# A two-block model on one NeuronCore: the order of high and low weight products in a unit

## What is computed

```python
u = hn @ e_w_in[j]                 # 2048 x 6144
mix = y @ e_w_out[j]               # 2048 x 2048
h = h + jax.nn.sigmoid(h @ ple_gate_w[i]) * pl
...
h = rms_norm(x, norm_g) @ w_in
return x + (y @ w_out).astype(x.dtype)
```

## Time and profile before

| | |
|---|---|
| median of 3 runs | 2110.85 us (2109.73 to 2111.03) |
| profiled execution | 2112.97 us |
| its span | 2111.2 us, 36924 instructions |
| TensorE busy, matmuls | 2087.3 us (99%), 11920 |
| weight loads | 1816.1 us (86%), 11920 |
| POOL busy | 1775.9 us (84%), 1393 |
| ACT busy | 1239.2 us (59%), 2221 |
| DVE busy | 1070.5 us (51%), 1848 |
| granted TensorE clock, mean | 0.997 |
| DMA | 377.72 MB, 179 GB/s in the mean |

### The profile page before, as it was taken

How to read it: one execution, slowest core, us unless ns; L and a number is a source line. 1 busy time by engine, 2 the same in 40 slices (tenths; PEclk the granted TensorE clock), 3 DMA queues, 4 the chain that set the end, 5 groups by cost and what they waited for, 6 DMA issues and landing times.

```text
span 2111.2 us, 36924 instructions
## 1 busy us (share of the span) xinstructions
PE 2087.3 (99%) x11920; PEld 1816.1 (86%) x11920; DVE 1070.5 (51%) x1848; ACT 1239.2 (59%) x2221; POOL 1775.9 (84%) x1393
## 2 busy tenths in 40 slices
PE   9999999999999999999999999999999999999997
PEld 8887888888888888888888988888888888878886
DVE  7567685345663256633466554405644651277612
ACT  6575457556555467765666465446655544476654
POOL 8799788999989987789898968897799889866786
PEclk9999999999999999999999999999999999999999
DMA  8555335555556554455566535564566656534464
GB/s 278 197 185 173 132 120 164 191 186 190 190 191 216 187 175 159 158 182 190 184 200 206 184 131 180 191 192 154 154 197 189 209 180 205 191 131 144 138 190 143
DMA packets 208226, 377.72 MB, mean 179 GB/s; under 512 B 23248, under 2 KB 29776, under 8 KB 207952
## 3 DMA queue, kind: packets, MB, share of 16 engines
q1 hardware_dynamic: 203904, 368.34, 54.3%
q10 hardware_dynamic: 4176, 7.53, 1.1%
HBM read 373.68 MB, written 2.10 MB: 178 GB/s over the span
## 4 chain that ended last, share of the span: by engine, by line
PE 82%; DVE 3%; POOL 1%; issue 0%; ACT 0%; ACTq 0%; DVEq 0%; POOLq 0%
PE ps L612 43%; PE ps L614 22%; PE ps L593 3%; PE ps L595 3%; PE ps L594 3%; PE ps L852 2%; PE ps L879 1%; POOL w_lo L516 1%; PE ps L864 1%; PE ps L602 1%; PE ps L604 1%; PE ps L603 1%; PE ps L811 0%; PE ps L584 0%; PE ps L801 0%
## 5 line engine op out<-in xcount | busy, mean ns | idle before, releaser
L516 POOL TENSOR_TENSOR w_lo<-raw,w_hi 128x512 fp32r<-128x512 f32 (+2 forms) x1370 | 1755.1, 1299 | 315.8 <-ACT w_hi L964 269.0
L964 ACT ACTIVATE w_hi<-raw 128x512 fp32r<-128x512 f32 (+1 forms) x1388 | 860.0, 627 | 737.7 <-PE ps L614 586.6
L612 PE MATMUL ps<-xa,w_hi 128*128 128x512 f32 x2576 | 882.1, 397 | 5.0 <-POOL w_lo L516 4.9
L612 PE MATMUL ps<-xb,w_hi 128*128 128x512 f32 x2016 | 704.2, 396 | 0.1
L614 PE MATMUL ps<-xa,w_lo 128*128 128x256 f32 x2576 | 661.9, 278 | 0.0
L614 PE MATMUL ps<-xb,w_lo 128*128 128x256 f32 x2016 | 553.6, 278 | 0.0
L612 PEld LDWEIGHTS ps<-xa,w_hi 128*128 128x128 f32 x2576 | 461.6, 188 | 91.2 <-issue 3.7
L614 PEld LDWEIGHTS ps<-xa,w_lo 128*128 128x128 f32 x2576 | 484.7, 188 | 29.9
L612 PEld LDWEIGHTS ps<-xb,w_hi 128*128 128x128 f32 x2016 | 377.4, 188 | 85.6 <-issue 0.6
L614 PEld LDWEIGHTS ps<-xb,w_lo 128*128 128x128 f32 x2016 | 379.0, 188 | 3.8
L1624 DVE TENSOR_SCALAR tb<-ps 128x512 f32<-128x512 f32 (+1 forms) x92 | 63.2, 687 | 253.0 <-PE ps L614 252.6
(11 more groups left out here) (372 smaller groups left out, 2124.7 us busy)
## 6 DMA issues: line engine op xcount, KB each, us to landing
raw<-w_gate_dram SPq DMA_DIRECT2D x128, 256.0 KB, 3.0
raw<-w_ogz_dram SPq DMA_DIRECT2D x128, 256.0 KB, 2.9
raw<-w_ein_dram SPq DMA_DIRECT2D x96, 256.0 KB, 3.1
raw<-w_evout_dram SPq DMA_DIRECT2D x80, 256.0 KB, 2.8
raw<-w_odin_dram SPq DMA_DIRECT2D x80, 256.0 KB, 3.0
raw<-w_odgate_dram SPq DMA_DIRECT2D x72, 256.0 KB, 2.8
raw<-w_einz_dram SPq DMA_DIRECT2D x64, 256.0 KB, 2.8
raw<-w_eout_dram SPq DMA_DIRECT2D x64, 256.0 KB, 3.0
```

Source lines behind the costliest of these rows:

```text
L516: nc.gpsimd.tensor_tensor(w_lo[:, slot, 0:n], raw[:, at, 0:n], w_hi[:, slot, 0:n].bitcast(F32), SUB).then_inc(lo_pool, 1)
L612: mm(ps[:, bank + b, :], w_hi[:, slot, at], x[:, x0 + k, :], start=(k == 0), stop=False)
L964: af(w_hi[:, slot, 0:n], raw[:, at, 0:n], ACT.Copy).then_inc(act_rounded, 1)
```

## The change

`halves_in_turn` keeps one order, pairs of cells, for every unit of every stage that asks for it. The lists LEAD and LEAD_UNITS are gone. The parameters p, q and units stay, p and units unused. Pairs are taken as two cells, not as nb cells: in odkey, which has nb 1, the two cells of a unit are (k, 0) and (k+1, 0), in the same bank. A unit of two cells (the smaller ones of odout) becomes high, high, low, low.

```diff
 HIGH, LOW = 0, 1
-LEAD = ((0, HIGH), (1, HIGH), (0, LOW), (2, HIGH), (1, LOW), (3, HIGH), (2, LOW), (3, LOW))
-LEAD_UNITS = {"ein": (16, 18), "eout": (0, 2, 8, 10), "gate0": (0, 2), "oqk": (0, 8, 10), "oout": (0, 2, 8, 10),
-              "gate1": (0, 2), "evc": (0, 8, 10), "evmem": (0, 2, 8, 10), "evgate_a": (10,),
-              "evmoba": (0, 2, 8, 10), "odin": (0, 2, 8, 10), "odmem": (0, 8, 10), "odgate": (32, 34, 56)}
-
-
 def halves_in_turn(st, p, q, units):
 
     cells = range(len(st.units[q]))
-    if len(units) < 4:
-        turns = [cells[k:k + st.nb] for k in range(0, len(cells), st.nb)]
-        return [(c, half) for turn in turns for half in (HIGH, LOW) for c in turn]
-    chunk = units[0] > 0 or len(units) < st.upp or st.name in ("evgate_a", "evgate_b")
-    listed = isinstance(p, int) and p * st.upp + q in LEAD_UNITS.get(st.name, (0,))
-    lead = listed or chunk and q == units[0]
-    return LEAD if lead and len(cells) == 4 else [(c, half) for c in cells for half in (HIGH, LOW)]
+    turns = [cells[k:k + 2] for k in range(0, len(cells), 2)]
+    return [(c, half) for turn in turns for half in (HIGH, LOW) for c in turn]
```

## The result

The changed kernel takes 2116.52 us in the median of six executions (2114.88 to 2119.86), the kernel before 2110.03 (2109.73 to 2111.03): a ratio of 1.0031, with an interval of 1.0021 to 1.0042. Measured once more over more executions it is 2115.77 against 2109.99, a ratio of 1.0026 (1.0017 to 1.0034). So the change costs 5.8 to 6.5 us by the medians, where 2.5 were forecast. The profiled execution after took 2114.88 us.

The account below looks back on a forecast made before the run. TensorE's own pace was taken as the bound. Nine long stretches (+1.5 us) and the short ones (+1.0) gave +2.5 us on the median of 2110.85: 2113.4 us, range 2110.5 to 2118.5.

Parts of the forecast that it names:

- the restarts: Openings of stretches after fp32 matmuls: the first two highs stand 0.19 or 0.08 us further apart, unchanged by the change.
- the nine long stretches: Stretches with 2520 highs, 630 units: 877.67 us before, 879.15 us forecast in pair order, so +1.5 us.
- the rival of the long rhythm: Pairs run at 1413 ns a unit in some long stages, 1.1 to 1.8 us more per stretch; chance 0.22.
- free order: Rival: a matmul's own size alone sets the distance; time stays at 2110.85 us or falls to 2106.7; chance 0.15.
- the forecast's own range: With 1393.3 ns a unit throughout, 2112.0 to 2115.0 us for the whole kernel; chance of this forecast 0.63.
- the term of evout: The stretch with evout, 352 highs, falls from 124.36 us by 1.6 us to 122.8 in pair order.
- the chunks: Short stretches: 24 of 4 in ogz +0.4 us, 15 of 8 +0.35, eight of 4 in odgate -0.2.

Follow-up runs that it names:

- the two taken again: The kernel before and the changed kernel, each run again unchanged for a second profile: 2110.2 us and 2115.77 us.
- the two kernels with the moved unit: The kernel before and the changed kernel, each with one einz unit moved ahead of the product TensorE waited for: 2108.37 us and 2113.62 us.
- fours: The changed kernel with four highs and then four lows in every unit: 2125.02 us, ratio 1.0069.
- the third kernel with the move: The kernel before with one einz unit moved, and plain order in ein from its third pair, einz and evc: 2108.8 us, ratio 0.9998.
- the kernel that is plain in all 146: The kernel before with its 146 paired units of ein, einz and evc put into plain order, lead-ins kept: 2109.91 us, ratio 0.9999.

## Why the prediction was right and wrong

**Right.** TensorE's pace is the bound; POOL, the waits and the restarts stayed; two highs on one bank cost nothing extra; a unit in pairs takes 1393 ns in every stage, on xa and xb, written out or in a register loop; the nine long stretches took 879.2 us together, where 879.15 were forecast. No stretch of pairs fell into another rhythm in any of the five profiles that have pairs throughout. So the rival of the long rhythm didn't happen, nor did a free order. The direction was right. That 2116.5 lies in the range of 2110.5 to 2118.5 is luck: the forecast's own range ended at 2115.0, and the upper part was there for pairs in the long rhythm, which didn't come. More than 2115.1 us had a chance of 0.23, for that same reason, and came for another.

**Wrong: the term of evout, -1.6 us, and the base it was credited to.** The step reads: "One of them, the one with evout (352 highs, 124.36 us), falls by 1.6 us to 122.8". It does fall to 122.8. But only in the profile before did it stand at 124.36; typically it stands at 122.27 and rises by 0.5. The prediction took the gain from one execution and added it to the median of others that didn't have that loss to give back. The text had the means to see it: it noted that the profiled execution was 2.12 us above the median and didn't ask what those were. Those were evout's 2.1 us and a fall of the clock, some 1.5, against a median of three that itself stood 1.4 above an execution without either (two of the three took over 2110.8); that 2.12 and evout's 2.1 are nearly equal is chance. With evout at 1387 ns the same sum is 2.5 + 2.1 = 4.6 us.

**Mis-sized: the chunks.** For chunks of 8 and 4 the sum had +0.35, +0.4 and -0.2, together 0.55 us. Between the first two profiles these 47 stretches give 0.9, between the two taken again 0.8, between the two kernels with the moved unit 1.1. Ogz's 24 give 0.5 in all three; those of 8 give 0.6, 0.4 and 0.6; odgate's -0.2, -0.15 and 0, since which of its chunks stand in the longer rhythm before the change differs from profile to profile. That makes 4.8 to 5.2 out of 4.6, and by length all the stretches that changed order give 4.8 between the two profiles taken again and 5.1 between those with the moved unit.

**What remains** of the first measurement's 6.5 us is in part the clock: four of the six executions after have a mean clock of 0.997, against 30 of 75 of the kernel before in the later series. One of them took 2119.86 us, more than a fall explains; it wasn't profiled. Each such fall costs about 1.5 us. Whether the changed kernel has them more often isn't settled: in the second measurement it was 5 of 11. With the clock up in both, the distance is 5.3 us, and the stretches above are all but a few tenths of it.

**The free order** isn't borne out as a mechanism: if a matmul's own size alone set the distance, every order would take the same, and the same eight matmuls take 1387 or 1413 ns in plain order, 1393 in pairs and 1403 in fours. Why, these runs don't show.

## What to carry to other kernels

Before a sum is made, ask what lies between the profiled execution and the median: a gain in a stretch that only the profile has lost is no gain. Where one engine is busy all the time, measure the distance between starts in long undisturbed stretches for each order that the program already holds; here that gave the long stretches of the changed kernel to a few hundredths of a us. A short idle time of TensorE can cost more than its length when the clock falls behind it, and covering it makes the times steadier too.

## What the runs showed of the hardware that was not expected

The pace of a fixed sequence of matmuls can have more than one rhythm. Plain alternation of 512 and 256 columns ran at 1386.7 or 1413.3 ns for eight, kept the one it had over the 56 to 88 units of each long stretch, and had either in two executions of one program. Two highs and two lows showed one rhythm only, 1393.3 ns, in five profiles. A unit of another order (high, high, low, high, low, high, low, low) at the start of a stage steers the plain order into the short one in all but one of 45 long stretches: without it, 13 us are lost over the kernel (2122.65 against 2109.73). What in the array makes the rhythm wasn't tried.

TensorE's clock fell from 2.4 to 1.2 GHz for 3.4 us behind an idle time of 1.86 us in some executions and not in others of the same program; with one unit moved into that place and 0.66 us idle ahead of it, neither profile shows a fall, and all 22 executions of the two kernels have a mean clock of 0.998. Of the third kernel with the move, ten of eleven have 0.998 and one, at 2116.18 us, 0.996: the move doesn't rule out every fall. With 1.73 us idle (the kernel that is plain in all 146) it was 11 of 11 with 0.998 too, so these runs don't tell whether the length of the idle time decides or something else that changed with it. The kernel before with one einz unit moved is the quickest found: 2108.37 us, a ratio of 0.9992 (0.9983 to 1.0001) to the kernel before, which the interval doesn't quite tell from none.
